# Two transformer blocks on one core: first joining level of a triangular inverse in 32x32 products, odd times first in the spectrum, first loads and the output in parts

## The chip, the cores and the metric

The kernel runs on one NeuronCore of a Trainium2 chip, as one program and one launch. The metric is the time of that launch on the device in microseconds (us). Five engines work side by side: PE (TensorE, the matmuls), DVE (VectorE), ACT (ScalarE), POOL (GpSimd) and SP (SyncE), which issues most of the DMAs. Each runs its own instruction list in order, and they meet at semaphores.

## What is computed

The reference applies two blocks, one after the other, to one sequence x of 512 positions and 1024 channels, all in float32. The parts that the change touches are these:

```python
def _gated_delta_rule(q, k, v, beta, g):      # per head and direction, chunks of c = 64
    a_mat = jnp.where(strict, jnp.einsum("bhnid,bhnjd->bhnij", kb, k) * decay, 0.0)
    a_mat = a_mat + jnp.eye(c, dtype=q.dtype)
    sol = lax.linalg.triangular_solve(a_mat, rhs, left_side=True, lower=True,
                                      unit_diagonal=True)
...
def _fft_conv(z, kspec):
    zs = jnp.fft.rfft(z, n=2 * l, axis=1)
    return jnp.fft.irfft(zs * kspec[None], n=2 * l, axis=1)[:, :l]
...
def first_block(...):                         # x = x + mixer; x + cross attention; x + swiglu, twice
    h = rmsnorm(x, norm_mix_g[layer])
    ...
def second_block(...):
    for i in range(DEPTH):                    # DEPTH = 2
        x = x + 0.5 * _swiglu(...)
        proj = _rmsnorm(x, mix_norm[i]) @ w_in[i]
        o_dn = _deltanet_group(...)           # 4 heads, both directions, calls _gated_delta_rule
        o_hy = _hyena_group(...)              # two _fft_conv in sequence
        x = x + jnp.concatenate([o_dn, o_hy], axis=-1) @ w_out[i]
        x = x + 0.5 * _swiglu(...)
    return _rmsnorm(x, final_norm)
```

## The kernel before, in words

The whole work is one hand-written list of stages. Each engine has its own program, which walks through the stages, so that the order on each engine is the order of the code, and no scheduler moves anything.

**Linear layers.** Weights come as units of 128x2048 numbers (1 MB) from `wall` into the two buffers `RAW`. ACT writes the high part into `WH` (L1789), DVE the rest into `WL` (L2282, `split_lo`), and PE makes three products for each 128x128 piece: `WH` by `HH`, `WH` by `HL`, `WL` by `HH` (L976 to L978), where `HH` and `HL` are the high and low parts of the activations (L1867 on ACT, L2480 on DVE). The accumulators are the two halves of PSUM, `ACC` and `MIX`, with four banks each.

**Start.** SP loads x (`X`, 2 MB) and then the weight units; POOL's queue loads `PAR` (gains), `CON` (constants), `MEM` and `POOLW`. PE runs `keep_clock`, 62 products of ones that no one reads, and then waits. The first norm is applied late: the first block of products runs on x times its gain, and the sum of squares (`sum_paired`, L1143) is taken by PE in the middle of the second block, before the scale is applied.

**Delta stage** (once per layer of the second block, `pe_delta`). The inverse of a unit triangular matrix is built by joining. DVE solves all diagonal blocks of 32x32; they go through DRAM (`blocks_out`, SP L893, 16 DMAs, eight for heads 0 and 1, then eight for heads 2 and 3) into `XI` and `XIT`, where `turn_blocks` on DVE (L2888, L2889) turns them. Level 0 joins blocks of 32 to 64, level 1 joins 64 to 128. A level is `left` (PE; ACT copies the result to `YS`, L2073), `right` and `right_turned` (PE), whose corners DVE keeps negated in `XI` and `XIT` (`corner`, L2892). Level 1 is done in products of 64x64, level 0 in products of 128x128, of which only the corners of 32x32 are kept. The names in parentheses are (pair of heads, head in the pair, level). Pair 0 is joined by itself. The joining of pair 1 is interleaved in PE's order with the recurrence of pair 0 over its four chunks: `values`, `update`, `output` on PE, the copy `UB` on DVE (L2926), `UBE` on ACT (L2086), the state `ST` on DVE (L2930 to L2936).

**Hyena stage.** The signal is turned (`ZT`), its spectrum is made by products with cosine and sine tables `FWK` for the even times (p = 0) and the odd times (p = 1), in two halves of the frequencies (fc). ACT copies the odd part into `T` (L2184), DVE adds and subtracts it from the even part (`combine`, L3057, L3058), multiplies with the filter (L3065 to L3071), and PE goes back (`inverse`, L1621).

**End.** The last norm: squares on ACT and DVE, sum on PE (L1143), root, scale (`late_scale`, L1150), eight DVE operations on `X` (L2512), and one DMA of 2 MB to the output (`y`).

## Time and profile before

| | |
|---|---|
| median of 3 runs | 3889.28 us (3885.48 to 3892.35) |
| the profiled execution: its own time | 3895.01 us |
| its span in the trace | 3893.2 us |
| PE busy / DVE / ACT / POOL, share of the span | 97% / 52% / 28% / 2% |
| share of PE in the chain that ended last | 88% |
| granted TensorE clock, mean | 0.984 of full speed |

The page is made from one execution. "Busy" is the time in which an engine had an instruction in flight, and PE's matmuls overlap, so its busy share is no measure of peak. The timeline merges instructions of one line into one row: "x32" with 3.74 us is the time from the first start to the last end. A float32 product gives two records on PE, so 16 products stand as x32. A bracket at the end of a row is the idle time of the engine before it and what ended it.

### The profile page before, as it was taken

Reading aid. Unit: us, or ns where it says so; the run is one execution under the profiler, and the core shown is the slowest. Engines: PE = TensorE matmul, PEld = TensorE weight load, DVE = VectorE, ACT = ScalarE, POOL = GpSimd, SP = SyncE. Lnnn points to the kernel's source line nnn. Section 1 sums busy time; section 2 is a strip of 40 time slices with the busy share of each in tenths; the row PEclk is TensorE's granted clock in tenths of the full one; section 3 lists DMA queues with packets and bytes.
Section 4 is the critical chain, followed back from the end, with each engine's and each line's share of the span. In section 5 each row is a group of like instructions: output and inputs, shape, how many; then the busy total and the mean of one; then the engine's idle time right before and its main releaser. Section 6 shows DMA issues by size and latency. Waiting matters only on the chain.

```text
span 3893.2 us, 43107 instructions
## 1 busy us (share of the span) xinstructions
PE 3761.5 (97%) x17694; PEld 3053.7 (78%) x17694; DVE 2042.6 (52%) x2512; ACT 1093.3 (28%) x1193; POOL 68.4 (2%) x81
## 2 busy tenths in 40 slices
PE   9999999989999999999999999999999998999997
PEld 8878888856778877888777678888888876878886
DVE  5565434463654435443765664434443766665443
ACT  3242222242432223222243222222222242322221
POOL 0000000000000000000110000000000002000000
PEclk9999999998999999999999999999999999999998
DMA  3222223110222222222312222222222313112221
GB/s 136 98 75 88 97 90 108 61 39 27 84 96 95 99 93 76 97 92 103 136 39 84 87 76 97 97 90 97 96 94 100 130 64 98 66 67 96 97 92 71
DMA packets 66788, 343.01 MB, mean 88 GB/s; under 512 B 23524, under 2 KB 23524, under 8 KB 30816
## 3 DMA queue, kind: packets, MB, share of 16 engines
q1 hardware_dynamic: 60864, 303.19, 22.0%
q0 software_dynamic: 5792, 37.92, 2.6%
q8 instruction: 99, 1.62, 0.2%
q14 instruction: 33, 0.27, 0.0%
HBM read 324.31 MB, written 16.78 MB: 88 GB/s over the span
## 4 chain that ended last, share of the span: by engine, by line
PE 88%; DVE 8%; ACT 2%; issue 1%; DMA 1%; SPq 0%; DVEq 0%; ACTq 0%
PE ACC L976 25%; PE ACC L978 25%; PE ACC L977 25%; PE ACC L1621 1%; DVE WL L2282 0%; DVE PT L3065 0%; DVE PT L3067 0%; DMA RAW<-wall 0%; PE MIX L1150 0%; DVE HL L2480 0%; PE MIX L1676 0%; PE MIX L1416 0%; PE MIX L1143 0%; PE ACC L1365 0%; PE ACC L1351 0%
## 5 line engine op out<-in xcount | busy, mean ns | idle before, releaser
L976 PE MATMUL ACC<-HH,WH 128*128 128x512 f32 (+1 forms) x3322 | 1306.8, 393 | 24.5 <-issue 9.2
L977 PE MATMUL ACC<-HL,WH 128*128 128x512 f32 (+1 forms) x3322 | 1290.1, 388 | 0.0
L978 PE MATMUL ACC<-HH,WL 128*128 128x512 f32 (+1 forms) x3322 | 1289.9, 388 | 0.0
L2282 DVE TENSOR_TENSOR WL<-RAW,WH 128x2048 fp32r<-128x2048 f32 x292 | 668.2, 2288 | 478.2 <-ACT WH L1789 478.0
L976 PEld LDWEIGHTS ACC<-HH,WH 128*128 128x128 f32 x3322 | 626.0, 188 | 171.1 <-issue 26.7
L977 PEld LDWEIGHTS ACC<-HL,WH 128*128 128x128 f32 x3322 | 626.6, 189 | 131.3 <-issue 5.6
L978 PEld LDWEIGHTS ACC<-HH,WL 128*128 128x128 f32 x3322 | 626.1, 188 | 129.9
L1789 ACT ACTIVATE WH<-RAW 128x2048 fp32r<-128x2048 f32 x292 | 556.6, 1907 | 595.7 <-PE ACC L978 589.0
L2380 DVE TENSOR_TENSOR SG<-ACC,RS 128x512 f32<-128x512 f32 x132 | 91.3, 692 | 628.6 <-PE ACC L978 628.4
L976 PE MATMUL ACC<-HIDH,WH 128*128 128x512 f32 x1056 | 410.8, 389 | 0.0
L977 PE MATMUL ACC<-HIDL,WH 128*128 128x512 f32 x1056 | 410.8, 389 | 0.0
L978 PE MATMUL ACC<-HIDH,WL 128*128 128x512 f32 x1056 | 410.8, 389 | 0.0
L1826 ACT ACTIVATE SG<-SG 128x512 f32<-128x512 f32 x132 | 83.6, 634 | 1060.8 <-DVE SG L2380 1060.8
L977 PEld LDWEIGHTS ACC<-HIDL,WH 128*128 128x128 f32 x1056 | 198.2, 188 | 41.5
L978 PEld LDWEIGHTS ACC<-HIDH,WL 128*128 128x128 f32 x1056 | 198.2, 188 | 41.1
L976 PEld LDWEIGHTS ACC<-HIDH,WH 128*128 128x128 f32 x1056 | 198.2, 188 | 40.9
L2373 DVE SCALAR_TENSOR_TENSOR X<-ACC,X 128x1024 f32<-128x1024 f32 x48 | 58.4, 1224 | 169.0 <-PE ACC L978 169.0
L1867 ACT ACTIVATE HH<-X,PAR 128x512 fp32r<-128x512 f32 x96 | 61.5, 711 | 148.0 <-DVE X L2373 120.1
L2386 DVE TENSOR_TENSOR T<-T,SG 128x512 f32<-128x512 f32 x132 | 91.5, 693 | 16.8 <-ACT SG L1826 2.1
L2389 DVE TENSOR_TENSOR HIDL<-T,HIDH 128x512 f32 (+1 forms) x132 | 91.4, 692 | 15.2
L983 PEld LDWEIGHTS ACC<-ONES 128*128 128x128 f32 x672 | 84.4, 206 | 15.1 <-ACT T L2099 5.7
L983 PE MATMUL ACC<-ONES 128*128 128x128 f32 x672 | 85.8, 290 | 7.8 <-ACT T L2099 4.1
(507 smaller groups left out, 2977.6 us busy)
## 6 DMA issues: line engine op xcount, KB each, us to landing
RAW<-wall SPq DMA_DIRECT2D x261, 1024.0 KB, 4.7
RAW<-wall SPq DMA_DIRECT2D x24, 768.0 KB, 4.1
KR<-spectra POOLq DMA_DIRECT2D x4, 2048.0 KB, 9.1
x_kept<-X POOLq DMA_DIRECT2D x2, 2048.0 KB, 7.0
FWK<-mats POOLq DMA_DIRECT2D x4, 1024.0 KB, 5.5
spectra<-SQ POOLq DMA_DIRECT2D x8, 512.0 KB, 3.0
spectra<-T POOLq DMA_DIRECT2D x8, 512.0 KB, 3.8
X<-x_kept POOLq DMA_DIRECT2D x2, 2048.0 KB, 14.1
```

The lines of the kernel that those rows point to most:

```text
L976: pe.matmul(out_ap, wh, hh, start=first, stop=False)
L977: pe.matmul(out_ap, wh, hl, start=False, stop=False)
L978: return pe.matmul(out_ap, wl, hh, start=False, stop=last)
L983: pe.matmul(bank[:, 0:P], ONES[:], ONES[:], start=True, stop=True)
L1789: act.activation(WH[n % 2][:], RAW[n % 2][:], ACT.Copy).then_inc(w_hi, 1)
L1826: act.activation(SG[:], SG[:], ACT.Silu).then_inc(silu_ready, 1)
L1867: act.activation(HH[:, c, :], X[:, c, :], ACT.Copy, scale=par(st.gain, c)).then_inc(h_hi, 1)
L2282: v.tensor_tensor(WL[n % 2][:], RAW[n % 2][:], WH[n % 2][:], ALU.subtract).then_inc(w_lo, 1)
L2373: v.scalar_tensor_tensor(x2, two, st.scale, x2, ALU.mult, ALU.add).then_inc(block_done, 1)
L2380: v.tensor_tensor(SG[:], two[:, 0, :], scale, ALU.mult).then_inc(gate_ready, 1)
L2386: step(v.tensor_tensor(T[:, j, :], T[:, j, :], SG[:], ALU.mult))
L2389: v.tensor_tensor(HIDL[:, bass.ds(off, 1), :], T[:, j:j + 1, :], HIDH[:, bass.ds(off, 1), :], ALU.subtract).then_inc(hid_ready, 1)
```

## The change

Nine things change, in four places.

- Start: SP loads `PAR`, half of the first weight unit, chunks 0 and 1 of x, the other half, chunks 2 and 3, chunks 4 to 7. `CON` and `MEM` are issued by POOL only when the loads before them have landed. ACT loads its table with a one-column activation. ACT and DVE split the first unit in two halves, the second half between the second and third chunk of x. `keep_clock` has 26 products in place of 62.
- Delta stage, level 0: `left`, `right` and `right_turned` take only the corners, in products of 32x32, twice as many of them.
- Hyena stage: the spectrum makes the odd times first; ACT copies them as two pieces of 128x512 while PE makes the even times; DVE waits for both. Before the second spectrum of a layer the odd times are also turned first, with a semaphore step of their own.
- End: 15 and 12 `keep_clock` products stand before the last sum and the last scale, the small copy behind the last norm is gone, and the output leaves in four DMAs of 512 KB, each after two of the eight operations.

```diff
@@ sync
-            sp.dma_start(X[:], xT).then_inc(x_landed, 16)
+            sp.dma_start(PAR[:], params).then_inc(par_landed, 16)
+            sp.dma_start(RAW[0][:, 0:8 * P], wall[0:1, :, 0:8 * P]).then_inc(half_landed, 16)
+            sp.dma_start(X[:, 0:2, :], xT[:, 0:2, :]).then_inc(x_landed[0], 16)
+            sp.dma_start(RAW[0][:, 8 * P:], wall[0:1, :, 8 * P:]).then_inc(w_landed[0], 16)
+            sp.dma_start(X[:, 2:4, :], xT[:, 2:4, :]).then_inc(x_landed[1], 16)
+            sp.dma_start(X[:, 4:8, :], xT[:, 4:8, :]).then_inc(x_landed[2], 16)
...
-            sp.dma_start(out, X[:]).then_inc(out_done, 16)
-            sp.wait_ge(out_done, 16)
+            for k in range(KD // 2):
+                sp.wait_ge(out_ready, k + 1)
+                sp.dma_start(out[:, 2 * k:2 * k + 2, :], X[:, 2 * k:2 * k + 2, :]).then_inc(out_done, 16)
@@ tensor, first block
+                            if first_unit:
+                                pe.wait_ge(half_lo, 1)
...
+                                    if first_unit and k == 4:
+                                        pe.wait_ge(w_lo, 1)
@@ tensor, last norm
+                    if st.gain == "final2":
+                        keep_clock(MIX[:, 2, :], 15)
                     sum_paired(st)
...
+                    if st.gain == "final2":
+                        keep_clock(MIX[:, 2, :], 12)
                     late_scale(st)
@@ tensor, delta
+                def joined(d, lev):
+
+                    w = (32, 64)[lev]
+                    return [(slice(o + w * d, o + w * d + w), slice(o + w - w * d, o + 2 * w - w * d)) for o in ((0, 64), (0,))[lev]]
...
-                            if lev == 0:
-                                mm = pe.matmul(ACC[:, 2 * a + d, c * P:c * P + P], DT[:, h, d, c, :], XI[:, d, TC * h + c, :], start=True, stop=True)
...
+                            for near, far in joined(d, lev):
+                                mm = pe.matmul(ACC[far, 2 * a + d, columns(c, near)], DT[near, h, d, c, far], XI[near, d, TC * h + c, near],
+                                               start=True, stop=True)
@@ tensor, hyena
-                signal_spectrum(0, 0)
+                signal_spectrum(0, 1, (0, 1)).then_inc(hy_so, 1)
                 pe.wait_ge(dn_oc, 4 * L + 4)
                 head_scales(1, MIX[:, 0:2])
-                signal_spectrum(0, 1).then_inc(hy_sp, 1)
+                signal_spectrum(0, 0, (0, 1)).then_inc(hy_sp, 1)
...
-            keep_clock(ACC[:, 0, :], 62)
-            pe.wait_ge(par_landed, 32)
+            keep_clock(ACC[:, 0, :], 26)
@@ scalar
+                    if st.b0 == 0 and c in (0, 2, 4):
+                        act.wait_ge(x_landed[c // 2], 16)
+                    if st.b0 == 0 and c == 2:
+                        act.wait_ge(w_landed[0], 16)
+                        act.activation(WH[0][:, 8 * P:], RAW[0][:, 8 * P:], ACT.Copy).then_inc(w_hi, 1)
...
-                        act.wait_ge(hy_sp, 2 * n + fc + 1)
+                        act.wait_ge(hy_so, 2 * n + fc + 1)
...
-                        act.activation(T[:], bank[:, 1:4:2, :], ACT.Copy).then_inc(hy_odd, 1)
+                        for cs in range(2):
+                            odd = act.activation(T[:, cs, :], bank[:, 2 * cs + 1, :], ACT.Copy)
+                        odd.then_inc(hy_odd, 1)
```

On SP the order of the program's first loads is this, before and then in the change (`RAW_52` and `RAW_53` are the two buffers `RAW`):

```order
L854 DMA X<-xT 128x4096
L868 DMA RAW_52<-wall 128x2048
L868 DMA RAW_53<-wall 128x2048
```

```order
L861 DMA PAR<-params 128x105
L862 DMA RAW_52<-wall 128x1024
L863 DMA X<-xT 128x1024
L864 DMA RAW_52<-wall 128x1024
L865 DMA X<-xT 128x1024
L866 DMA X<-xT 128x2048
L882 DMA RAW_53<-wall 128x2048
```

One load of x and one of the first unit have become five, and the gains `PAR` stand ahead of them; the second unit (`RAW_53`) is now seventh.

On PE, in the first delta stage, from the first `left` to the first recurrence step's `update` (`SQ,DQ`), before and then in the change. Products are given with rows by columns of the weights' side:

```order
L1326 MATMUL ACC<-XI,DT 128x128 x16
L983 MATMUL MIX<-ONES 128x128 x10
L1340 MATMUL ACC<-YS,XIT 128x128 x16
L1351 MATMUL ACC<-XIT,YS 128x128 x16
L1329 MATMUL ACC<-XI,DT 64x64 x16
L1354 MATMUL ACC<-XIT,YS 64x64 x16
L1365 MATMUL ACC<-XIT,KG 128x128 x16
L1377 MATMUL MIX<-DQ,XIT 128x128 x4
L1326 MATMUL ACC<-XI,DT 128x128 x8
L1397 MATMUL MIX<-SQ,DQ 128x128 x4
L1326 MATMUL ACC<-XI,DT 128x128 x8
L1416 MATMUL MIX<-AT,SQ 128x128 x4
```

```order
L1358 MATMUL ACC<-XI,DT 32x32 x32
L998 MATMUL MIX<-ONES 128x128 x10
L1370 MATMUL ACC<-YS,XIT 32x32 x32
L1382 MATMUL ACC<-XIT,YS 32x32 x32
L1358 MATMUL ACC<-XI,DT 64x64 x16
L1382 MATMUL ACC<-XIT,YS 64x64 x16
L1393 MATMUL ACC<-XIT,KG 128x128 x16
L1405 MATMUL MIX<-DQ,XIT 128x128 x4
L1358 MATMUL ACC<-XI,DT 32x32 x16
L1425 MATMUL MIX<-SQ,DQ 128x128 x4
L1358 MATMUL ACC<-XI,DT 32x32 x16
L1444 MATMUL MIX<-AT,SQ 128x128 x4
```

Nothing has moved; each group of 128x128 at level 0 is now twice as many products of 32x32, and the groups of 64x64 and the `keep_clock` (`MIX<-ONES`) between them are as they were.

On ACT, the start of the program, before and then in the change (`WH_54` and `WH_55` are the two buffers `WH`):

```order
L1789 ACT_TABLE_LOAD
L1789 ACTIVATE WH_54<-RAW_52 128x2048
L1867 ACTIVATE HH<-X,PAR 128x512 x8
L1789 ACTIVATE WH_55<-RAW_53 128x2048
```

```order
L2303 ACT_TABLE_LOAD
L2303 ACTIVATE PRE<-ONES 128x1
L2305 ACTIVATE WH_54<-RAW_52 128x1024
L1900 ACTIVATE HH<-X,PAR 128x512 x2
L1899 ACTIVATE WH_54<-RAW_52 128x1024
L1900 ACTIVATE HH<-X,PAR 128x512 x6
L1818 ACTIVATE WH_55<-RAW_53 128x2048
```

The table load stands before any wait for data, and the second half of the first unit comes between chunks 1 and 2 of x.

## Rows read from the trace of the kernel before

**Rows 1.** The page, part 1: busy time, share, instructions.
```profile
PE 3761.5 (97%) x17694; PEld 3053.7 (78%) x17694; DVE 2042.6 (52%) x2512; ACT 1093.3 (28%) x1193; POOL 68.4 (2%) x81
```

**Rows 2.** Timeline, first 60 us: start us, us, engine, line, operation [idle before <-releaser].
```profile
1.10 15.57 PE L983 MATMUL ACC<-ONES 128*128 128x128 f32 x124 [1.10 <-DVE ONES L3105]
...
13.56 1.28 ACT L1789 ACT_TABLE_LOAD   x1 [13.56 <-DMA RAW<-wall]
...
16.90 2.29 DVE L2282 TENSOR_TENSOR WL<-RAW,WH 128x2048 fp32r<-128x2048 f32 x1 [15.86 <-ACT WH L1789]
19.11 5.39 DVE L2480 SCALAR_TENSOR_TENSOR HL<-X,PAR,HH 128x512 fp32r<-128x512 f32 x8
...
20.00 0.47 PE L976 MATMUL ACC<-HH,WH 128*128 128x512 f32 x1 [3.33 <-DVE HL L2480]
...
32.63 0.69 DVE L2455 TENSOR_TENSOR SQ<-SQ 128x512 f32<-128x512 f32 x1
```

**Rows 3.** Chain that ended last, first 60 us: start us, us, what.
```profile
20.47 0.23 PE ACC L977
...
38.18 0.79 PE MIX L1143 x8
```

**Rows 4.** The page, part 6: DMA issues, KB each, median us to landing.
```profile
RAW<-wall SPq DMA_DIRECT2D x261, 1024.0 KB, 4.7
RAW<-wall SPq DMA_DIRECT2D x24, 768.0 KB, 4.1
```

**Rows 5.** Timeline of PE in the first delta stage.
```profile
2088.55 8.14 PE L983 MATMUL ACC<-ONES 128*128 128x128 f32 x56 [2.03 <-ACT T L2099]
2096.53 3.74 PE L1326 MATMUL ACC<-XI,DT 128*128 128x128 f32 x32
...
2110.93 0.68 PE L1329 MATMUL ACC<-XI,DT 64*64 64x64 f32 x16 [0.67 <-DVE XIT L2892]
...
2117.02 1.06 PE L1377 MATMUL MIX<-DQ,XIT 128*128 128x128 f32 x8
...
2137.66 0.68 PE L1329 MATMUL ACC<-XI,DT 64*64 64x64 f32 x16
2138.27 0.71 PE L1411 MATMUL MIX<-E,ST 128*128 128x128 f32 x4
```

**Rows 6.** Timeline of DVE in the first delta stage.
```profile
2099.65 0.67 DVE L2889 STREAM_TRANSPOSE XI<-XIT 128x512 f32<-128x512 f32 x1
2104.33 1.19 DVE L2892 TENSOR_SCALAR XI<-ACC 32x128 f32<-32x128 f32 x4 [4.01 <-PE ACC L1340]
```

**Rows 7.** Timeline of ACT in the first delta stage.
```profile
2119.22 0.60 ACT L2086 ACTIVATE SQ<-MIX 128x512 f32<-128x512 f32 x1 [0.97 <-DVE SQ L2926]
```

**Rows 8.** One window: length, busy PE, PEld, DVE, ACT, POOL (instructions), PEclk, DMA, GB/s.
```profile
2090.00:2092.00 2.00, 2.00 (x11) 2.00 (x11) 0.00 (x0) 0.00 (x0) 0.00 (x0) 0.50 1.01 351
```

**Rows 9.** Timeline of DVE in the second delta stage.
```profile
3300.84 0.71 DVE L2888 STREAM_TRANSPOSE XIT<-XI 128x512 f32<-128x512 f32 x1 [6.48 <-DMA XIT<-blocks_out]
```

**Rows 10.** Timeline of PE in the second delta stage.
```profile
3309.72 0.68 PE L1329 MATMUL ACC<-XI,DT 64*64 64x64 f32 x16 [0.67 <-DVE XIT L2892]
```

**Rows 11.** Timeline of ACT and DVE in the first hyena stage.
```profile
2182.97 0.63 ACT L2138 ACTIVATE HH<-DQ 128x512 fp32r<-128x512 f32 x1 [0.75 <-DVE DQ L2995]
...
2185.43 1.23 DVE L3057 TENSOR_TENSOR ZS<-ACC,T 128x1024 f32<-128x1024 f32 x1 [1.10 <-ACT T L2184]
...
2229.85 1.22 DVE L3057 TENSOR_TENSOR ZS<-ACC,T 128x1024 f32<-128x1024 f32 x1 [5.67 <-ACT T L2184]
```

**Rows 12.** Timeline, last microseconds.
```profile
3873.83 1.87 PE L1143 MATMUL MIX<-ONES,SQ 128*128 128x1 f32 x8 [4.39 <-DVE SQ L2455]
...
3877.98 2.07 PE L1150 MATMUL MIX<-T,ONES 128*128 128x512 f32 x2 [2.28 <-DVE T L2469]
3880.09 6.23 DVE L2512 SCALAR_TENSOR_TENSOR X<-X,PAR,MIX 128x512 f32<-128x512 f32 x8 [2.17 <-PE MIX L1150]
```

**Rows 13.** DMA issues of the last microseconds.
```profile
y<-X SPq DMA_DIRECT2D x1, 2048.0 KB, 6.2
```

More of the change, by code:

```diff
@@ L497, in build @@
         rs_at = (nc.sbuf_usable_end - 4 * S) // 32 * 32 - 4 * S
-        assert low + 4 * 2 * KF * S <= rs_at
+        PRE = place("PRE", [P, 1], at=low + 4 * 2 * KF * S)
+        assert low + 4 * 2 * KF * S + 32 <= rs_at
         EV_YA = put("EV_YA", [P, 4, S])
@@ L561, in build @@
         par_landed = sem("par_landed")
-        x_landed = sem("x_landed")
+        con_landed = sem("con_landed")
+        half_landed = sem("half_landed")
+        half_hi = sem("half_hi")
+        half_lo = sem("half_lo")
+        x_landed = [sem(f"x_landed{i}") for i in range(3)]
         mem_landed = sem("mem_landed")
@@ L1337, in right @@
                     if lev == 0:
-                        for d in range(2):
-                            for c in range(TC):
-                                mm = pe.matmul(ACC[:, 2 * a + d, c * P:c * P + P], XIT[:, d, TC * h + c, :], YS[:, a, d, c, :], start=True, stop=True)
+                        for c in range(TC):
+                            for d in range(2):
+                                for near, far in joined(d, lev):
+                                    mm = pe.matmul(ACC[far, 2 * a + d, columns(c, near)], XIT[far, d, TC * h + c, far], YS[far, a, d, c, near],
+                                                   start=True, stop=True)
                         mm.then_inc(dn_t, 1)
@@ L1546, in signal_turned, with signal_spectrum @@
                     mm.then_inc(hy_zt, 1)
-                def signal_spectrum(fc, cs):
+                def signal_spectrum(fc, p, css):
                     bank = (ACC, MIX)[fc]
-                    for p in range(2):
+                    for cs in css:
                         for kc in range(2):
@@ L2465, in dve_diag @@
                 inverse_root(MIX[:, 0, 0:TC], RN[:, 0, :], TC, P * st.n)
+                if st.b0 == 0:
+                    v.wait_ge(con_landed, 16)
                 h = st.h0 + (st.n if st.late else 0)
```

86 lines of the change are left out of this document (51 added, 35 removed).

## The prediction

> **What bounds the kernel now.** I read the page first: PE is busy 97% of the span [rows 1], so over most of the program only less PE work or a shorter PE wait is worth anything, and the triples of large products are not touched. So I looked at the four places of the change alone, each by the timeline of PE and then of the engines that it waits for.
>
> At the start PE runs products of ones until 16.7 us and then idles until 20.00, when the first low part `HL` is there [rows 2]. Behind that stands a chain without slack: data landed at 13.56, the table load of 1.28, the split of the first unit on ACT (till 16.8) and DVE (2.29), and 0.67 for one chunk of `HL` (5.39 for 8) [rows 2]. So the start is bound by loads and then by a serial preparation.
>
> In the joining of pair 0, PE, ACT and DVE hand work to each other. The four groups of corners on DVE start at 2104.33 and PE waits for the last of them at 2110.93 [rows 5, 6]. In the joining of pair 1 PE never idles. In the second layer the same place is late for another reason: DVE waited 6.48 us for the DMA of heads 2 and 3, to 3300.84, and has four transposes of 0.6 each to do before it can keep the first corner, so not before 3303.3 [rows 6, 9]. In the first layer they were done at 2100.3 [rows 6].
>
> In the hyena stage `combine` begins at 2185.43 and 2229.85, each time released by ACT's copy `T` [rows 11], and the DVE chain behind it is what PE waits for. At the end all is serial.
>
> **Start.** One 256 KB more costs a load 0.6 us (4.7 against 4.1), so a load is 2.3 us and 2.4 us per MB [rows 4]. With issue at about 1 us, the half unit lands at 4.7, x chunks 0 and 1 at 5.9, the other half at 7.1, chunks 2 and 3 at 8.3, the rest of x at 10.7. ACT's split of a whole unit lay between 14.84 and DVE's start at 16.90, so half takes 1.0; DVE's half takes 1.15, `HL` 0.67, gaps 0.3: the first product could go at 7.8. `keep_clock` is now 52 records of 0.126 (15.57 for 124 [rows 2]) and ends at 7.6. I take 8.0 in place of 20.0: 12.0 us. Chunk 2 of x then waits for the second half: landed 8.3, ACT 1.0, DVE 1.15, then `HL` 0.67 and gaps: 11.7, while PE is through two chunks at 8.0 + 12 x 0.23 = 10.8 [rows 3]; I charge 0.9. From 20.00 to the sum at 38.18 are 72 products, 16.6 us at 0.23 [rows 3]; the missing 1.6 are products at the lower clock after the idle time, which the new order avoids. Start: 12.0 - 0.9 + 1.6 = 12.7. The sum also needs the squares, which were done at 33.32, 4.9 before PE came [rows 2, 3]; they hang on x's last chunks and on the second unit, the seventh load now, and shift by about 9, so the margin shrinks to about 1; if that unit lands 2 us later than I think, PE waits 1. `CON` and `MEM`, now later, are needed only behind the second block. Bounds: 10.5 if each landing is 1.5 us later, 13.5 if nothing waits at chunk 2.
>
> The moved waits: `PAR` now stands ahead of everything on SP's queue; nothing that it had to pass is needed earlier. POOL waits for x chunks 2 and 3 and for the second unit before it issues `CON` and `MEM`; behind it on POOL stand only loads for later stages. ACT waits for chunks of x with the second unit's split queued behind, which PE needs only for its second block, near 20 us.
>
> **Delta, the price of a call.** No product of 32x32 stands in the trace. The nearest row is the 64x64 group: 16 records take 0.61 until the next group starts, the changes of tile size included [rows 5]. A call at level 0 was 16 records in 1.79 (32 in 3.58, from 3.74 with the tail) and is now 32 records. Bounds: 0.61 if a small record costs half of a 64x64 one, 1.22 if it costs the same 0.038. I take 1.2 among large products and 0.9 where such calls follow one another.
>
> The Trainium skill (TensorE: Matmul & The Clock Gate, Part 1) states that start to start never falls below about 25 ns, for 32 columns too. By that page a call would be an estimated 0.8 and the changes of tile size beside it; the sum does not use this.
>
> **Delta, pair 0, first layer.** The two `left` calls save 1.3 (3.6 to 2.3, since the second one waits for its transposed blocks). The first `right` saves 0.9 before DVE can begin. Then DVE is the chain: four groups of 1.19 back to back are 4.9, where 6.6 passed [rows 5, 6]: 1.7. Together 3.9. The 20 records of `keep_clock` stay.
>
> **Delta, pair 0, second layer.** DVE cannot keep a corner before 3303.3. Four groups from there end at 3308.3, and level 1 can start at 3308.3 in place of 3309.72 [rows 10]: 1.4 only. PE is done with `right` at about 3300.3 and idles till 3304.6, 4 us. In the first delta stage an idle time of 2.03 before 2088.55 was followed by a window at half the full clock, 1.2 GHz, though PE was then dense [rows 5, 8]. So I expect PE at 1.2 GHz when it goes on, through most of the large products of `keys_solved` (3.6 at full clock): 3.3 lost with the small calls. Net -1.9; +1.4 if the clock holds.
>
> **Delta, pair 1, both layers.** Six calls save 0.6 each on PE, 3.6. But `update` needs the copy `UBE`. From the start of `values` at 2117.02 to the end of that copy at 2119.82 are 2.8 us, and `values` with a call filled them (0.9 + 1.8) [rows 5, 7]. The calls before the first and the second `update` were the cover of this wait, which is now bare: 1.3 of the 3.6 becomes waiting. 2.3 per layer remain. Queued behind that wait is all of PE. Bounds: 1.0 to 3.5.
>
> Delta in sum: 3.9 + 2.3 - 1.9 + 2.3 = 6.6.
>
> **Spectrum.** PE work is equal. In the second spectrum of a layer ACT's copy (1.1) leaves the path, and turning the odd times first starts `ZT` four records of 0.112 earlier: 1.6 (DVE has the filter ready by then, since it idled 5.67 before 2229.85). In the first spectrum ACT is busy with `HH` until 2183.60 and then copies two pieces in 1.1, so DVE can start at 2184.8 in place of 2185.43 [rows 11]: 0.6. Per layer 2.2, in sum 4.4. If the half pieces cost more on ACT, 3.5.
>
> **End.** The last sum takes 1.87 and the last scale 2.07 [rows 12], both at 1.2 GHz; at 2.4 GHz they are half of that, 0.9 and 1.0 less. The 30 records before the sum (0.112 each, 3.4) end before it and cost nothing; the 24 before the scale take 2.7 where 2.24 pass until DVE has the diagonal (end of L1143 to L1150 [rows 12]): 0.4 back. Net 1.5. If the clock falls all the same, the 24 records take 5.1 and the edit costs 2.9. The output: 2 MB took 6.2 [rows 13]; a last piece of 512 KB takes 3.5 by the rule of [rows 4], and the pieces before it have 1.6 us each, enough for 1.2. With the copy that is gone 2.9. End: 4.4.
>
> **The sum.** 12.7 + 6.6 + 4.4 + 4.4 = 28.1. The profiled execution took 3895.0, 1.8 more than its span, so it would take 3866.9. The runs' median lies 5.7 below the profiled one: 3861.
>
> **The rivals.**
> 1. Everything at full size: the DMA of heads 2 and 3 lands in time in layer two, as it did in layer one, or PE's clock holds: 3 to 6 more, 3856.
> 2. The small products don't overlap. The two blocks of one direction go to the same PSUM bank from different rows of the array, where the 64x64 groups alternate between two banks. If such records take turns, at 2 x 0.038, a call costs 2.4, 0.6 more than before. Pair 1 then costs 3.6 per layer and pair 0 some 2: delta -11, the time 3879. If only the gain is lost, delta is 0 and the time 3868. For it: no row has two row tiles in one bank. Against: small records kept up 38 ns wherever they stand in the trace. The Trainium skill (TensorEngine Tiling, Gotcha 1: PSUM Pressure) states that different row tiles cannot access the same PSUM bank simultaneously; no row of this trace shows it.
> 3. The loads share the queue and land together: the start gives 6 to 7, 3867.
> 4. The other side: PE runs the joinings at 1.2 GHz, since 32x32 products keep too little of it busy. One microsecond at 1.2 GHz costs half a microsecond; the 28 us are used up at 56 us of lower clock, 28 per layer, which is most of the 53 us of both joinings. At 50 per layer: 3911. Against: large products stand between the calls, and 64x64 groups held full clock.
>
> **Chances.** Forecast 0.55, rival 1 0.20, rival 2 0.10, rival 3 0.11, rival 4 0.04. The range takes in rivals 1 and 3 and of rival 2 the case without gain. Its low end is rival 1 with the best bounds of start and calls (0.8 and 2 x 1.2, and some 4 from the clock), its high end the forecast with 10.5 at the start, pair 1 at 1.0 and 4.4 lost at the end as the clock and a whole-size landing would have it: 3849 to 3873. Changes below 0.2%, 7.8 us, are about what a measurement of this kernel cannot tell from none. Faster 0.96, same 0.015, slower 0.025.
>
> **What would show it.** In the trace after: first product of L976's successor near 8.0 and the sum at 25 to 26; 32 records of a level-0 call in 0.9 to 1.2; DVE's first corner in the second delta stage still after 3303 less what was won before it; a PEclk below full there; `combine` released by PE in the second spectra and by ACT in the first; the last scale near 1.0 us, the last DMA below 4. What would make the forecast wrong above all: the landing of the first half unit, and the price of a 32x32 record.

## The result, and the profile after

The changed kernel takes 3862.57 us (median of 4 runs, 3857.84 to 3865.31), where the one before took 3889.9 beside it: a ratio of 0.9926, with a 95% interval of 0.9913 to 0.994. Measured once more with the last experiments it took 3859.11 (5 runs, 3853.26 to 3865.63), ratio 0.9922 (0.9908 to 0.9935). The ratio on record is not the quotient of the two medians, which is 0.9930, and 0.9913 the second time; so ratios that differ by less than 0.001, some 4 us, are not told apart below. The profiled execution took 3864.46 with a span of 3862.7, and the span of the one before was 3893.2, so 30.5 us have to be found in the two traces. I lay the same products of both traces side by side (the start of each in before, less its start in after) and see where the difference steps.

| Part | forecast | found in the traces | why it differs |
|---|---|---|---|
| Start, up to the first sum | 12.7 | 10.5 | the first pieces of x land 2.4 later than forecast |
| Delta, pair 0 (both layers) | 2.0 | -2.0 | late in both layers, and not only in the second |
| Delta, pair 1 (both layers) | 4.6 | 11.6 | a call costs 0.38, not 1.2 |
| Spectrum (both layers) | 4.4 | 4.3 | (read against the undone edit, below) |
| End | 4.4 | 4.1 | the clock fell and took the 1.5 of the two products; the output gave more |
| Sum | 28.1 | 28.5 | the other 2.0 are steps up and down in stages that are the same |

The 2.0 are the balance of larger steps: some 1.6 gained between 122 and 134 us (granted clock from 120 to 140 us 0.91 before and 1.00 after), 3.6 lost near 900 (from 885 to 930 us 0.85 before and 0.71 after), and 4.3 gained in the hyena stages beyond the spectrum's 4.3.

Start of the changed kernel, timeline of ACT, DVE and PE (start us, us, engine, line, operation, [idle before <-releaser]), and then the sum in the chain that ended last. They answer to [rows 2, 3].

```profile
5.61 1.06 ACT L2305 ACTIVATE WH<-RAW 128x1024 fp32r<-128x1024 f32 x1 [3.36 <-DMA RAW<-wall]
...
8.27 1.34 ACT L1900 ACTIVATE HH<-X,PAR 128x512 fp32r<-128x512 f32 x2 [1.60 <-DMA X<-xT]
...
9.99 0.47 PE L991 MATMUL ACC<-HH,WH 128*128 128x512 f32 x1 [0.56 <-DVE HL L2524]
...
13.77 0.50 PE L991 MATMUL ACC<-HH,WH 128*128 128x512 f32 x1 [0.77 <-DVE HL L2524]
```
```profile
27.66 0.79 PE MIX L1166 x8
```

The first half unit landed just before 5.61 and x chunks 0 and 1 just before 8.27, so PE starts at 9.99 and not at 8.0; it waits 0.77 for chunk 2.

Pair 0 of the first delta stage, timeline of PE, DVE and POOL's DMA queue; it answers to [rows 5, 6].

```profile
2084.74 0.54 POOL L958 DMA_DIRECT2D KR<-spectra  x1 [3.89 <-DMA spectra<-T]
...
2085.92 0.45 SPq L907 DMA_DIRECT2D XIT<-blocks_out  x1
...
2088.16 0.81 PE L1358 MATMUL ACC<-XI,DT 32*32 32x32 f32 x64
...
2088.90 2.50 PE L998 MATMUL MIX<-ONES 128*128 128x128 f32 x20
...
2094.48 0.71 DVE L2937 STREAM_TRANSPOSE XIT<-XI 128x512 f32<-128x512 f32 x1 [7.22 <-DMA XIT<-blocks_out]
...
2097.00 2.41 DVE L2941 TENSOR_SCALAR XI<-ACC 32x128 f32<-32x128 f32 x8
2098.25 0.65 PE L1382 MATMUL ACC<-XIT,YS 32*32 32x32 f32 x32 [6.17 <-DVE XI L2941]
```

64 small records pass in 0.74 us, 11.6 ns each. But POOL issues the 2 MB of `KR` at 2084.74, and SP the last of the 32 KB block loads of heads 2 and 3 at 2085.92; the blocks are there 8 us later, DVE stands at them, and PE waits 6.17 for a corner that DVE could have kept at 2092. Before the change DVE waited 0.34 for the same blocks, and PE was busy meanwhile with whole products. Three rows of before, of DVE, POOL and SP's queue:

```profile
2097.83 0.71 DVE L2888 STREAM_TRANSPOSE XIT<-XI 128x512 f32<-128x512 f32 x1 [0.34 <-DMA XIT<-blocks_out]
```
```profile
2095.01 0.53 POOL L943 DMA_DIRECT2D KR<-spectra  x1 [5.68 <-DMA spectra<-T]
2095.04 0.45 SPq L893 DMA_DIRECT2D XIT<-blocks_out  x1
```

A window of PE in that stretch (length, busy, PEclk, DMA share, GB/s) shows the price behind the wait:

```profile
2095.00:2097.00 2.00, 0.00 (x0) 0.50 0.04 8
```

PE goes on at 1.2 GHz, and `keys_solved`, 3.84 at full clock, takes 5.39. Pair 1 on PE, between large products:

```profile
2111.40 0.45 PE L1358 MATMUL ACC<-XI,DT 32*32 32x32 f32 x32
2112.25 1.16 PE L1425 MATMUL MIX<-SQ,DQ 128*128 128x128 f32 x8 [0.40 <-DVE SQ L2975]
2113.34 0.45 PE L1358 MATMUL ACC<-XI,DT 32*32 32x32 f32 x32
2113.72 1.16 PE L1444 MATMUL MIX<-AT,SQ 128*128 128x128 f32 x8
```

A call is over 0.38 after its start (2113.34 to 2113.72) where 16 whole products took 1.79. The bared wait of `update` is there (0.40), three times in a layer. The last microseconds answer to [rows 12, 13]; the last row is of the view of the DMA issues.

```profile
3842.89 3.51 PE L998 MATMUL MIX<-ONES 128*128 128x128 f32 x30
...
3847.44 1.05 PE L1166 MATMUL MIX<-ONES,SQ 128*128 128x1 f32 x8 [1.04 <-DVE SQ L2492]
3848.35 4.55 PE L998 MATMUL MIX<-ONES 128*128 128x128 f32 x24
...
3852.74 1.02 PE L1173 MATMUL MIX<-T,ONES 128*128 128x512 f32 x2
3853.80 5.86 DVE L2556 SCALAR_TENSOR_TENSOR X<-X,PAR,MIX 128x512 f32<-128x512 f32 x8 [3.08 <-PE MIX L1173]
```
```profile
y<-X SPq DMA_DIRECT2D x4, 512.0 KB, 2.6
```

The 24 products of ones took 4.55 and not 2.7: the clock fell under them, and the scale came 2 us after its input `T` was there. From the start of the sum to the start of the operations on `X` it is 6.36 here and was 6.26 before, so the products of ones gained nothing in this execution. The 4.1 come from the tail behind the last operation (3.04 for 6.88) and from the eight operations themselves (5.86 for 6.23), which nothing in the prediction foresaw.

### The profile page after: what moved, and what is told of

Its sections match the earlier page's. It is cut to its first block, busy times and chain, and to the rows that moved or that the text cites. A ratio compares the mean times of both kernels' runs of the same rounds, so it can differ in the third digit from the quotient of the medians.

```text
span 3862.7 us, 43859 instructions
## 1 busy us (share of the span) xinstructions
PE 3728.6 (97%) x18060; PEld 3019.1 (78%) x18060; DVE 2042.4 (53%) x2512; ACT 1094.9 (28%) x1203; POOL 68.2 (2%) x80
## 4 chain that ended last, share of the span: by engine, by line
PE 86%; DVE 9%; ACT 2%; issue 1%; DMA 1%; SPq 0%; DVEq 0%; ACTq 0%
PE ACC L991 25%; PE ACC L993 25%; PE ACC L992 25%; PE ACC L1651 1%; DVE BX L2927 1%; DVE BT L2925 1%; DVE PT L3117 0%; DVE PT L3115 0%; DVE WL L2319 0%; DMA XIT<-blocks_out 0%; PE ACC L1393 0%; DVE HL L2524 0%; PE MIX L1706 0%; PE MIX L1769 0%; PE MIX L1173 0%
## 5 line engine op out<-in xcount | busy, mean ns | idle before, releaser
L2420 DVE TENSOR_TENSOR T<-ACC,RS 128x512 f32<-128x512 f32 x132 | 89.9, 681 | 0.0
```

The source lines that it names most:

```text
L2420: v.tensor_tensor(T[:, j, :], two[:, 1, :], scale, ALU.mult).then_inc(block_done, 1)
```

## The experiments

Each kernel is the changed kernel with the edit shown. "Pair 0" below is the time from the first `left` of a delta stage to `values` of pair 0.

### The four parts, one undone at a time

**The level in whole products.** Level 0 of `left`, `right` and `right_turned` with 128x128 slices as before:

```diff
-                            for near, far in joined(d, lev):
-                                mm = pe.matmul(ACC[near, 2 * a + d, columns(c, far)], YS[far, a, d, c, near], XIT[far, d, TC * h + c, far],
+                            if lev == 0:
+                                mm = pe.matmul(ACC[:, 2 * a + d, c * P:c * P + P], YS[:, a, d, c, :], XIT[:, d, TC * h + c, :], start=True, stop=True)
```

> The changed kernel with only the first joining level of the delta stages back in 128x128 products (16 records a call). Theory A (a call of 32 small records costs what the trace of the changed kernel shows, 0.38 to 0.45 us among large products, against 1.79 for 16 large ones): pair 1 of each delta stage loses some 5.8 us, pair 0 of the first layer gains back 1.9 (the clock fall there hid the saving), pair 0 of the second layer about 0: 7.7 to 12 us slower than the changed kernel, 3870 to 3875. Rival B (my prediction's own sizes, call 1.2): 6.6 slower, 3869. Rival C (the 5.8 in pair 1 came from something else, such as the clock): pair 1 differs by under 3 us from the changed kernel's and the time stays within 3 of 3863. In the trace: the stretch from keys_solved of pair 0 to the end of the delta chain in layer one was 32.73 before and 26.94 after pair 0 in the changed kernel; A says 32.7 again.

Measured: 3875.37 us, ratio 0.9952 (0.9936 to 0.9967). Pair 1 took 5.8 longer in each layer, as theory A had it, so the 11.6 of pair 1 are the small products. Pair 0 took 21.08 and 21.62, against 22.25 and 21.30 in the changed kernel, and 20.4 to 23.0 over the seven traces with its delta stage and the first loads in parts: there the small products gain nothing. The rows of DVE and PE say why:

```profile
2092.80 0.71 DVE L2939 STREAM_TRANSPOSE XIT<-XI 128x512 f32<-128x512 f32 x1 [6.87 <-DMA XIT<-blocks_out]
...
2096.57 3.84 PE L1382 MATMUL ACC<-XIT,YS 128*128 128x128 f32 x32 [0.32 <-DVE XI L2943]
```

The blocks are as late here, DVE waits as long, but PE waits 0.32 only: the whole products last just as long as the DMA. What the small ones save turns into waiting. The rivals with another cause of pair 1's gain fall.

**The start as before.** First loads, splits, waits and the 124 products of ones of the old start:

```diff
-            sp.dma_start(PAR[:], params).then_inc(par_landed, 16)
-            sp.dma_start(RAW[0][:, 0:8 * P], wall[0:1, :, 0:8 * P]).then_inc(half_landed, 16)
...
+            sp.dma_start(X[:], xT).then_inc(x_landed, 16)
...
-            keep_clock(ACC[:, 0, :], 26)
+            keep_clock(ACC[:, 0, :], 62)
+            pe.wait_ge(par_landed, 32)
```

> The changed kernel with only the order of the first loads and the first splits put back as before (output, delta and spectrum as changed). Theory A: the first sum of squares moves back from 27.66 to 38.2 us in the trace and the time grows by 10.5 to 12 us, to 3873 to 3875. Rival B: the start is worth less in the time than in the trace's first 40 us, because the clock of a later stage falls instead (the lead fell from 12.1 to 8.3 near 900 us in the two traces): 7 to 9 us, 3870 to 3872.

Measured: 3873.13 us, ratio 0.9951 (0.9935 to 0.9967), 10.6 and 14.0 above the two medians of the changed kernel. The time is theory A's, but its mark in the trace was missed: the first sum came at 36.64 and not at 38.2, so only 9.0 behind the changed kernel's 27.66. In this execution the clock stayed up behind the idle time (granted 1.00 from 20 to 26 us), where before the change it fell (0.50 from 22 to 24). At 155 us the distance was 10.6, but the 1.6 in between are a step of the clock (granted 0.91 from 120 to 140 us) that four of the twelve traces with the first loads in parts show as well. So the start is worth 9.0 when the clock holds behind the old start's idle time and 10.5 when it falls. The lead that shrank near 900 us was the clock of one execution (below).

**One output DMA.**

```diff
-                sp.dma_start(out[:, 2 * k:2 * k + 2, :], X[:, 2 * k:2 * k + 2, :]).then_inc(out_done, 16)
-            sp.wait_ge(out_done, 16 * KD // 2)
+            sp.dma_start(out, X[:]).then_inc(out_done, 16)
+            sp.wait_ge(out_done, 16)
```

> The changed kernel, but x leaves in one DMA after the last of the eight scalings instead of four DMAs, one behind every second scaling. Theory A: the last DMA of 2 MB takes 6.2 as it did before instead of the 2.6 to 3 of the last quarter: 3.0 to 3.6 us slower than the changed kernel, 3866. Rival B: the four parts overlap so well that they hide more than that, or each DMA's fixed part is what counts: under 1.5 us.

Measured: 3863.97 us, ratio 0.9925 (0.991 to 0.994). The time alone says rival B. The trace says A:

```profile
3850.26 5.86 DVE L2556 SCALAR_TENSOR_TENSOR X<-X,PAR,MIX 128x512 f32<-128x512 f32 x8 [3.10 <-PE MIX L1173]
3856.22 0.34 SPq L914 DMA_DIRECT2D y<-X  x1
```

DVE is done at 3856.12 and the span ends at 3862.9, 6.8 later; in the changed kernel it ends 3.0 behind DVE (3859.66 to 3862.7). That is 3.7 to 3.8 for the output in parts. The run's last sum was 3.6 earlier than in the changed kernel's trace for reasons of the clock, which covers it, and the interval of the ratio is 12 us wide. I take the trace's 3.7; the timed runs alone neither show it nor exclude it.

**The spectrum's order as before.**

```diff
-                signal_spectrum(0, 1, (0, 1)).then_inc(hy_so, 1)
+                signal_spectrum(0, 0)
...
-                        for cs in range(2):
-                            odd = act.activation(T[:, cs, :], bank[:, 2 * cs + 1, :], ACT.Copy)
+                        act.activation(T[:], bank[:, 1:4:2, :], ACT.Copy).then_inc(hy_odd, 1)
```

> The changed kernel with the spectrum's order as before: even and odd times together, ACT's copy T behind all of them. Theory A (my prediction): 2.2 us per layer, 4.4 slower, 3867. Rival B: the hyena stages of the two traces differ by 6.4 in layer one and 2.2 in layer two because the edit is worth more than I said, or because of the clock: if the edit, the time grows by 6 or more; if the clock, the hyena stage of this kernel's layer two, less the clock, differs by 2 to 2.5.

Measured: 3869.12 us, ratio 0.9943 (0.9928 to 0.9958). Two rows of the changed kernel, and behind them the same two of this one; they answer to [rows 11]:

```profile
2171.09 1.23 DVE L3107 TENSOR_TENSOR ZS<-ACC,T 128x1024 f32<-128x1024 f32 x1 [0.28 <-ACT T L2218]
...
2212.66 1.23 DVE L3107 TENSOR_TENSOR ZS<-ACC,T 128x1024 f32<-128x1024 f32 x1 [4.40 <-PE ACC L1639]
```
```profile
2173.38 1.23 DVE L3102 TENSOR_TENSOR ZS<-ACC,T 128x1024 f32<-128x1024 f32 x1 [1.10 <-ACT T L2215]
...
2216.20 1.23 DVE L3102 TENSOR_TENSOR ZS<-ACC,T 128x1024 f32<-128x1024 f32 x1 [5.67 <-ACT T L2215]
```

`combine` is released by ACT in the first spectrum and by PE in the second, as forecast. The lag of this kernel grows by 0.8 at each first spectrum and by 1.0 at each second, and by 0.2 and 0.4 where `ZT` starts the second one (2207.91 against 2205.39 in layer one): 2.1 and 2.2 a layer, 4.3 in all. What the two traces of before and after differ in beyond that (6.4 in the first hyena stage) is the clock: an `inverse` that takes 7.17 after took 8.76 before. The time alone would have said rival B: it is 6.6 and 10.0 above the two medians, where B asked for 6 or more. Its interval, 6 us to either side, also holds the 4.3, and I go by the trace.

The four ratios stand 0.0028, 0.0027, 0.0001 and 0.0019 above 0.9924, the mean of the changed kernel's two: in sum 0.0075, and the whole change is worth 0.0076. Each alone is uncertain by about 0.0015, so an agreement as close as this is chance; it shows only that no large part is missing.

### Why pair 0 is late

**The transposes behind the corners.** On DVE `turn_blocks(1)`, which waits for the DMA of heads 2 and 3, goes from its place ahead of `keep_right(0, 0)` to behind `keep_last(0, 1)`:

```diff
                 turn_blocks(0)
-                turn_blocks(1)
                 keep_right(0, 0)
...
                 keep_last(0, 1)
+                turn_blocks(1)
```

> The changed kernel with one call moved on DVE: the four transposes of heads 2 and 3, which wait for their DMA, now stand behind the last corner of pair 0 instead of ahead of its first one. Theory A: what PE waits 6.2 (layer one) and 7.0 us (layer two) for in pair 0 is DVE held at that DMA. PE then waits at most 2 us there, keys_solved of pair 0 starts 10.5 to 12.5 us behind the first small product instead of 17.0, the clock does not fall in the stage, and the time drops by 10 to 14 us, to 3849 to 3852. Rival B: the chain of corners and copies is what takes the time (its groups of 1.2 us) and the DMA only hides it: under 2 us per layer. Rival C: pair 1's products now wait for the transposes instead: PE waits for DVE's XIT or XI at the first 32x32 group of pair 1, and most of the gain is given back.

Measured: 3858.11 us, ratio 0.9913 (0.9898 to 0.9928), not the 3849 to 3852 of theory A. PE's wait is 1.02. Pair 0 takes 18.67 and 16.24, against 22.2 and 21.3 to 22.2 in the two traces of the changed kernel: 9 us in sum. Pair 1 takes 23.3 as before, so rival C falls, and B with it. But two things of theory A failed: the clock fell all the same, and in layer one there is a new wait.

```profile
2088.00:2090.00 2.00, 0.30 (x9) 1.00 0.77 234
2090.00:2092.00 2.00, 1.06 (x61) 0.50 0.03 3
```
```profile
2090.91 1.06 PE L1382 MATMUL ACC<-XIT,YS 32*32 32x32 f32 x61 [1.59 <-issue]
...
2097.35 5.19 PE L1393 MATMUL ACC<-XIT,KG 128*128 128x128 f32 x32
```

The first fence is PE's windows, the second its timeline. Three records of a call had gone when PE waited 1.59 for nothing that the profile shows, and the clock fell in that gap. The median lies 1.0 to 4.5 us under the changed kernel's, less than the traces show and less than A; the interval reaches the 9 of the traces and A's 10 only just.

**`KR` behind the blocks.** POOL waits for the blocks before it issues the 2 MB; DVE's order is as changed:

```diff
+                    pool.wait_ge(solved_landed[1], 128 * (l + 1))
                     pool.dma_start(KR[0][:], spectra[0]).then_inc(kf_back[0], 16)
```

> The changed kernel with one wait added on POOL: the 2 MB load of KR is issued only when the inverse blocks of heads 2 and 3 have landed. DVE's order is as changed. Theory A: the blocks are late because they share the DMA engines with the 2 MB; alone they land about 2.5 us behind their issue, as those of heads 0 and 1 do, instead of 8; DVE's second transposes start near 2088.5 and PE's wait of 6.2 to 7.0 us shrinks to under 2, the time to 3849 to 3852, as with the transposes moved. Rival B: the blocks' DMAs are slow by themselves (eight small ones of many short rows each) and land at the same distance whether KR runs or not: no change, 3862.

Measured: 3856.53 us, ratio 0.9897 (0.988 to 0.9914), 2.6 and 6.0 under the two medians and again not A's 3849 to 3852. DVE, PE, and DMA issues of this run:

```profile
2084.24 0.71 DVE L2938 STREAM_TRANSPOSE XIT<-XI 128x512 f32<-128x512 f32 x1 [0.37 <-DMA XIT<-blocks_out]
...
2089.35 0.45 PE L1383 MATMUL ACC<-XIT,YS 32*32 32x32 f32 x32 [1.02 <-DVE XI L2942]
```
```profile
XIT<-blocks_out SPq DMA_DIRECT2D x1, 32.0 KB, 2.0
```

The blocks land 2.0 us behind their issue, where the changed kernel has

```profile
XIT<-blocks_out SPq DMA_DIRECT2D x3, 32.0 KB, 7.8
```

DVE waits 0.37 and not 7.22. Pair 0 takes 16.12 and 16.35, 11 us less in sum, and the ratio falls by 0.0025 to 0.0029, 10 to 11 us. Against the kernel before (20.49 and 21.18) that is 4.4 and 4.8: with the blocks in time pair 0 gives somewhat more than the 3.9 that I had forecast for it in the first layer. So the 2 MB on POOL's queue are why the block loads on SP's queue are late. This is theory A's cause; B falls. The Trainium skill (DMA: Bandwidth & Descriptors, SWDGE vs HWDGE vs iDMA) states that the two paths feed different queues inside each DMA engine and that the engine serves them by turns. The trace agrees in that both queues move at once: 2249 packets of 120 bytes beside 144 packets of 15 KB in the 11 us from 2084. That a small packet waits there for large ones is my inference; no row shows the turns themselves.

### The price of a small record

**Sixteen in a row to one bank.** The loops of both levels in another order:

```diff
-                    for c in range(TC):
-                        for d in range(2):
+                    for d in range(2):
+                        for c in range(TC):
                             for near, far in joined(d, lev):
```

> The changed kernel with the loops of both joining levels in another order: direction outside, blocks of time inside, so that a call's 16 small records in a row go to one PSUM bank instead of two and two by turns. Theory A: small products in different rows and columns of the array do not disturb each other in a bank: a call of 32 records still takes 0.38 until what follows and 64 records 0.75. Rival B (my rival 2): products in one bank take turns: the call grows to 0.6 or more.

Measured: 3867.13 us in one run. Pair 1 on PE:

```profile
2110.23 0.60 PE L1358 MATMUL ACC<-XI,DT 32*32 32x32 f32 x32
2110.76 1.16 PE L1444 MATMUL MIX<-AT,SQ 128*128 128x128 f32 x8
```

A call takes 0.53 and not 0.38, and a 64x64 call 0.90 (2122.61 to 2123.51) and not 0.61: 4.7 ns more a record in the small ones, far from the 38 of my rival 2. Neither theory had this. From `values` to `keys_solved` of pair 1 it is 24.8 for 23.3.

But this edit changes two things and not one. With the direction outside, sixteen records in a row go to one bank, and they also use fewer tiles of the array: the 32x32 products go by turns to two tiles where four took turns, and four 64x64 products in a row go to the same tile where two took turns. Records that overlap less because they share a tile would be slower in the same way, and no run separates the two. The Trainium skill (TensorEngine Tiling, Gotcha 1: PSUM Pressure) states that different row tiles cannot access one PSUM bank at the same time. The sign fits that, and it fits the tiles as well. What the run does show is that the changed kernel's order, with another bank and another tile after two products at most, is worth about 1.5 us a layer, and that a full turn of 38 ns for each record does not come.

### The first loads

**The half unit alone.**

```diff
             sp.dma_start(RAW[0][:, 0:8 * P], wall[0:1, :, 0:8 * P]).then_inc(half_landed, 16)
+            sp.wait_ge(half_landed, 16)
```

> The changed kernel in which SP waits for the first half unit (512 KB) before it issues any other load. Theory A: the first load is slow because DMA is slow in the first microseconds whatever is under way: it lands at 5.2 to 5.6 as now, and x and the rest come later, so the first sum moves from 27.7 to 29 or later. Rival B: it shares the DMA engines with the x chunks behind it: alone it lands at 4.0 to 4.7, where I had put it.

Measured: 3860.79 in one run; the half unit landed at 5.08, between A and B. In the two traces of the changed kernel it was 5.61 and 5.47, so sharing costs it 0.4 to 0.5, and the other 0.4 over the forecast 4.7 have another reason. The sum came 1.7 later.

**The whole unit in the half's place.**

```diff
-            sp.dma_start(RAW[0][:, 0:8 * P], wall[0:1, :, 0:8 * P]).then_inc(half_landed, 16)
+            sp.dma_start(RAW[0][:], wall[0:1, :, :]).then_inc(w_landed[0], 16)
             sp.dma_start(X[:, 0:2, :], xT[:, 0:2, :]).then_inc(x_landed[0], 16)
-            sp.dma_start(RAW[0][:, 8 * P:], wall[0:1, :, 8 * P:]).then_inc(w_landed[0], 16)
```

> The changed kernel with the first weight unit loaded whole (1 MB in rows of 8 KB) where its first half (512 KB in rows of 4 KB) stood, and no second half; the splits stay in halves. Theory A: the rows of 4 KB are what makes the first loads slow (176 to 295 GB/s until 7 us, against 400 and more with 8 KB): the whole unit lands at 6.3 or before, only 0.7 behind the half, chunk 2 waits less, and the first sum stays at 27.2 to 28. Rival B: the first microseconds are slow whatever the rows: it lands at 7.3 or later, the first product goes at 11.5 or later, and the first sum at 28.5 or later.

Measured: 3853.18 in one run. Timeline of ACT and PE, then a window of this kernel and behind it the same window of the changed one (us, busy PE, PEld, DVE, ACT, POOL, PEclk, DMA share, GB/s):

```profile
6.08 1.06 ACT L2304 ACTIVATE WH<-RAW 128x1024 fp32r<-128x1024 f32 x1 [3.83 <-DMA RAW<-wall]
...
10.05 0.47 PE L990 MATMUL ACC<-HH,WH 128*128 128x512 f32 x1 [0.85 <-DVE HL L2523]
```
```profile
3.00:5.00 2.00, 2.00 (x11) 2.00 (x11) 0.00 (x0) 0.00 (x0) 0.00 (x0) 1.00 0.89 373
```
```profile
3.00:5.00 2.00, 2.00 (x11) 2.00 (x11) 0.00 (x0) 0.00 (x0) 0.00 (x0) 1.00 0.97 231
```

1 MB in rows of 8 KB lands 0.5 behind 512 KB in rows of 4 KB. The engines are as busy in both and move 373 GB/s in the one and 231 in the other. The x chunks that PE waits for land no earlier (8.33), so the first product goes no earlier (10.05, against 9.99 and 9.52 in the two traces of the changed kernel); the wait at chunk 2 is gone, and the sum comes 1.0 earlier (26.47 against 27.50 in the timeline; 27.09 in the second trace). Theory A, by one execution: the halves cost what they were to save. That this one execution took 3853 is not from the start; its lead grows from 1.0 to 7.0 in stages that are the same (below).

### The end

**More products of ones ahead of the sum.**

```diff
-                        keep_clock(MIX[:, 2, :], 15)
+                        keep_clock(MIX[:, 2, :], 19)
```

> The changed kernel with 38 instead of 30 products of ones ahead of the last sum of squares, so that PE's idle time of 1.04 us before it goes. Theory A: it is that idle time after which the clock fell in three of five traces (24 products took 4.2 to 4.55 us), and not in two (2.92): the 24 products take 2.9 and the last scale starts 1.1 us behind the start of T. Rival B: the fall is caused by the sum's eight one-column products and comes all the same in some executions; one trace that shows 4.2 to 4.6 proves B, one that shows 2.9 leaves it open.

Measured: 3863.51 in one run.

```profile
3843.50 4.40 PE L998 MATMUL MIX<-ONES 128*128 128x128 f32 x38
3848.05 1.05 PE L1166 MATMUL MIX<-ONES,SQ 128*128 128x1 f32 x8
3848.96 2.92 PE L998 MATMUL MIX<-ONES 128*128 128x128 f32 x24
3851.72 1.02 PE L1173 MATMUL MIX<-T,ONES 128*128 128x512 f32 x2
```

The idle time is gone and the clock held, here and in the combined kernel below. In the eleven traces with the idle time of 1.04 it fell in five (24 products in 4.2 to 4.6) and held in six (2.92). Two that held against six of eleven is a hint that the idle time is what lets it fall, not more. When the clock holds, the sum to the end of the span is 13.6 (3837.87 to 3851.5 in the second trace of the changed kernel) and not 15.3.

### All together

**Combined**: the transposes behind the corners and the 38 products of ones ahead of the sum, as above, and products of ones in the gaps of pair 0:

```diff
+                keep_clock(MIX[:, 0, :], 4)
                 right_turned(0, 0, 0)
+                keep_clock(MIX[:, 0, :], 3)
                 right_turned(0, 1, 0)
+                keep_clock(MIX[:, 0, :], 2)
                 left(0, 0, 1)
```

> The changed kernel with the transposes of heads 2 and 3 behind pair 0's last corner, 38 products of ones ahead of the last sum, and in pair 0 of each delta stage 8, 6 and 4 products of ones in the gaps of 1.02, 0.77 and 0.68 us that the run with the moved transposes showed behind the first right call and the two right_turned calls. Theory A: with these gaps filled the clock holds in pair 0: keys_solved takes 3.84 instead of 4.6 to 5.2 and the 64x64 groups no longer run at half clock; pair 0 takes 11 to 12 us from the first small product instead of 13.6 (layer one) and 11.8 (layer two), and the time falls to 3851 to 3855. Rival B: the clock falls all the same (the 32x32 groups themselves keep too little of PE busy), and the fillers only add their overrun: no better than the run with the moved transposes alone, 3856 to 3860. Either way faster than the changed kernel and the one before.

Measured: 3853.83 us (3851.92 to 3859.43), ratio 0.9906 (0.9891 to 0.9921), as theory A had it. Timeline of PE in layer one:

```profile
2092.91 0.82 PE L998 MATMUL MIX<-ONES 128*128 128x128 f32 x5 [2.23 <-issue]
...
2095.93 1.43 PE L1358 MATMUL ACC<-XI,DT 64*64 64x64 f32 x32
```

The clock held in pair 0 of both layers: the 32 records of 64x64 take 1.43 and not 2.34, `keys_solved` takes 3.84. Pair 0 is 17.22 and 15.13. Layer two is the best of all kernels; layer one lost 2.23 to the same wait for nothing that the profile shows, 0.89 of it in layer two. This kernel has the lowest median of those with more than one run, 5 to 9 us under the changed kernel's, and the one with `KR` behind the blocks the lowest ratio; their intervals overlap, so I can't say which is faster. Both beat the kernel before.

**The changed kernel again.**

> The changed kernel itself, unchanged, beside the others on one chip: its ratio to the kernel before was 0.9926; both theories expect 0.991 to 0.994. Its trace shows whether the late landing of heads 2 and 3 in pair 0 (about 8 us, PE waits 6 to 7) and the steps of 1.5 to 2 us of the clock in untouched stages come again: theory A says the first does in every execution and the second moves about.

Measured: ratio 0.9922. Pair 0 took 22.18 and 22.24, with waits of 6.16 and 6.17 for DVE: the late blocks come every time. But this execution took 3853.26, 11 less than the first one profiled. Windows of the untouched stretch, the first profiled execution and then this one:

```profile
890.00:900.00 10.00, 10.00 (x15) 4.38 (x15) 2.09 (x2) 4.67 (x9) 0.00 (x0) 0.50 0.00 0
```
```profile
890.00:900.00 10.00, 10.00 (x49) 6.54 (x47) 2.09 (x3) 4.55 (x9) 0.00 (x0) 1.00 0.00 0
```

PE was at 1.2 GHz for all of the ten microseconds in one and at 2.4 in the other, in the same code. The mean granted clock was 0.984 and 0.987, and 3862.7 x 0.984 and 3851.5 x 0.987 are 3801 both, to the 2 us that three digits of the clock allow.

## Why the prediction was right, and where its steps were not

The forecast was 3861 and the range 3849 to 3873; the two medians are 3862.57 and 3859.11. That the sum was this close is luck: the parts are off by -2.2 (start), +7.0 (pair 1), -4.0 (pair 0) and -0.4 (spectrum and end), and only together by +0.4.

- **Start (12.7; it was 10.5).** Of its steps the chain on ACT and DVE held, and the wait at chunk 2 (0.77 idle, about 1.1 until products run at their pace again, for 0.9). What failed is "a load is 2.3 us and 2.4 us per MB": that came from rows with the queue in full flow and 8 KB rows. The first half unit landed at 5.6 (4.7), x chunks 0 and 1 at 8.3 (5.9), and these, not the weights, released PE. The whole-unit run points at rows of 4 KB as the cause for a good part of the first. The 1.6 from the lower clock came (the 72 products and the wait took 17.67 where 18.18 passed before), but they are the clock of one execution of the kernel before: with the old start put back it held, and the start was worth 9.0.
- **The price of a call (1.2 or 0.9; it was 0.38).** It lay outside my bounds, 0.61 to 1.22. I took one end because the bound was "the same 0.038 a record". The lower one assumed a small record to cost half of a 64x64 one; it costs 11.6 ns, less than a third. The Trainium skill (TensorE: Matmul & The Clock Gate, Part 1) states a start to start of never below about 25 ns; these records, in different tiles of the array, contradict it. Part 3 of the same page, on matmuls in different tiles that overlap with starts some 4 ns apart, is nearer to what the trace shows, though 11.6 is not 4.
- **Pair 1 (2.3 a layer; it was 5.8).** Mis-sized by the call above all. The bared wait is there at three updates, not two: 0.40, 0.47 and 0.40. From its rows: three calls end in such a wait and save 0.9 each, three save 1.4; 7.0 in sum, less some 1.2 as the large products behind a wait or a change of tile start later by 0.1 to 0.2.
- **Pair 0, first layer (3.9; it was -1.9).** The step that failed is that DVE had its transposes done at 2100.3, before the change. That was so by a narrow margin: POOL issued `KR` at 2095.01 and SP its last block load at 2095.04. In every other delta stage that was traced, both layers, with the orders of POOL and DVE as changed or as before, `KR` was issued at least 0.19 ahead of that load and DVE waited 6.5 or more for the blocks. Why `KR` comes relatively earlier there, no run shows. I had read in layer two just this mechanism and took layer one for safe.
- **Pair 0, second layer (-1.9; it was -0.1).** The mechanism was right, DVE held by its transposes, PE idle for 7.0 us at 3286.89, the clock down behind it. In this execution `keys_solved` ran at full clock (3.84); in the second trace it took 5.43 and the term was -1.1. The 3.3 that I had charged for the clock were so too much: what ran low in both is the 64x64 groups (32 records in 2.34, and 1.43 in the combined kernel, where the clock held).
- **Spectrum (4.4; 4.3).** Right in each step: 0.8 for 0.6 at the first and 1.3 to 1.4 for 1.6 at the second.
- **End (4.4; 4.1).** The output and the copy that is gone gave 3.8 for 2.9, and the eight operations 0.4 that I did not have. The clock fell under the 24 products (4.55, for the 5.1 of my conditional), but that did not cost the 2.9 that I had written down: the two edits of products came out at -0.1, since the sum and the scale took 1.05 and 1.02 all the same, for 1.87 and 2.07 before. When the clock holds they give the 1.5 of the forecast, and the end is worth 5.7.

Of the rivals, the first came about in part: the blocks never landed in time, but `keys_solved` ran at full clock or nearly (3.84 to 3.92) in four of the sixteen pair 0 stretches of the eight traces that have the changed kernel's delta stage. Of the second, sixteen records in a row to one bank and to half as many tiles cost 4.7 ns each, and nothing that I can see is lost in the order chosen. The third did not come: the half unit is 0.4 to 0.5 late by sharing, and the start gave 10.5 and not 6 to 7. The fourth did not come: between large products the full clock held through pair 1, and in pair 0 it fell behind PE's idle time.

Open: what PE waited for in the 1.59 and 2.23 us of "issue". It came in the two kernels where PE reached `right_turned` while `KR` was on its way, and a fetch of instructions stands on the DMA queues in the same stretch; but it does so in the run where `KR` waited, too, and no wait came. No run separates it. Whether bank or tile slows the small records when the order is changed is open, too. Removing the 24 products at the end was not tried.

## What to carry to other kernels

A stage that "hides" a wait stops hiding it when it is made faster: look at what the engine next door waits for in that stretch, and put the large transfer that is not yet needed behind the small ones that are. Price the record in small matmuls by how many stand in tiles and banks of their own, not by the last size that stands in the trace; which of the two counts, tile or bank, these runs do not say. Two traced executions of one program differ here by 11 us through the clock in stages that nobody touched, and timed runs of the kernel before lie between 3884.82 and 3904.36, so an edit of 3 us is read from its own stretch of the trace and not from the total.

## What the runs showed of the hardware that I had not expected

- 32x32 records in different tiles start 11.6 ns apart (64 in 0.74 us), and 16.6 when sixteen in a row go to one PSUM bank and to two tiles in place of four; 64x64 records 38 with two tiles by turns, and 56 with one bank and one tile.
- 512 KB in rows of 4 KB and 1 MB in rows of 8 KB land within 0.5 us of each other at the start of the program (5.6 and 6.1, one execution each).
- A 2 MB load on POOL's queue makes loads of 32 KB on SP's queue, issued after it, land in 7.8 us instead of 2.0.
- An idle time of 1.04 us was followed by a falling clock in five of eleven traces of the same stretch of code.
